# First attention of a hybrid decoder layer: values as weights in two column halves, probabilities weighed by GpSimd

## The chip, the cores and the metric

One Trainium2 chip, one core of it. The time is device microseconds of one launch; the kernel before has a median of 715.19 us over three runs (712.88 to 716.78). An engine is named as the profile names it: PE is TensorE's matrix products, PEld its weight loads, DVE is VectorE, ACT is ScalarE, POOL is GpSimd, SP is the engine whose queue issues most loads.

## The reference, cut to what matters

One decoder layer on 512 tokens of width 1024, float32. Two attention mixers read one input projection. Group 0 is a latent attention (MLA): 8 heads, head size 96 for scores and 64 for values, causal. Group 1 is a sparse attention (NSA) with a compressed, a selected and a windowed branch. Each group's 512 output features are RMS-normalised over the features of a token, both are multiplied with an output matrix and added to the residual; a squared-ReLU MLP of width 4096 follows.

```
s = einsum('bqhd,bkhd->bhqk', qi, k) * scale
p = masked_softmax(s, pos[None, :] <= qpos[:, None])
o_a = einsum('bhqk,bkhd->bqhd', p, v)            # MLA, 8 heads of 64
mix = concatenate([rms_norm(o_a, grp_norm_mla), rms_norm(o_b, grp_norm_nsa)])
x = x + mix @ w_o
h2 = rms_norm(x, ln2_g)
x = x + square(relu(h2 @ w_up)) @ w_down
```

## The kernel before, in words

The 512 tokens are four tiles of 128 (t = 0 to 3). All of the work is written out by hand for each engine, in one list per engine, with semaphores between them; nothing is scheduled by a planner. A `Signal` counts what is done, and `wait_ge(*signal.at(key))` waits for the one of that key.

Attention runs as a list of units, one unit for one query tile and one head. Units 0 to 31 are the first attention (`N_MLA = 32`; tile 0 with heads 0 to 7, then tile 1, and so on; a unit of tile t has (t+1) times 128 keys). Then come the units of the second attention; unit 32 + u is called step u here, and steps 0 to 15 are the selected and the windowed branch of query tile 3. Each engine walks over the units in a loop with index n, and does for several units at a time one stage of each:

- PE computes the score of unit n (L1630 for the first attention, L1641 and L1642 for the second), queries on partitions, keys along the row, in banks S.
- DVE adds the mask and finds the row minimum, into `s_buf` (`low_unit`, L1108), with two banks and two buffers in turn.
- ACT takes the exponential into `p_buf` and sums the row into `den` (`exp_unit`, L759), one unit later.
- PE turns the probabilities, 128 keys at a time, into a bank T (`turn_unit(n - 2)`, L1463, the same line that records every transpose).
- DVE (odd units) or ACT (even units) copies the bank into `pt_buf` (`pt_out(n - 3)`, L1118 and L769).
- PE multiplies with the values (`mix_unit(n - 4)`, L1669). The turned probabilities are the weights (keys by 128 queries) and the 64 value columns of the head are what moves; the result has queries on partitions, 8 heads beside one another in a bank O.

A float32 product is two records each of PEld and PE in the trace (transposes are one). When the eight heads of a query tile are done, DVE divides by the row sums and writes `o_mla` (`out_row("mla", t)`, L1129 to L1140).

Among the units of the first attention stand other jobs: the last projections of the second attention (`project`, L1442 to L1444, 27 units), its head norms (`norm_in` on ACT, `nsa_sum` on DVE, a power on POOL at L473 and L476, `nsa_row` and `nsa_turned` on DVE), and copies into high and low parts (`act_lo` L1224, `q_pairs` L1232). A float32 matrix is kept as two float32r parts, high and low, for dense products.

The two attentions are two loops on each engine. PE's first loop goes on for four rounds after its last score to empty its stages (L1678), and only then does the second loop begin (L1778); ACT and DVE have the same seam.

In the second attention's time group 0 of the mix is finished: ACT squares and sums `o_mla` (L854), POOL takes the power and writes the scaled `mix_row` (L575), PE turns it by four transposes (`turn_mix(0, t)`, at steps 9, 15, 20 and 23), ACT and DVE split it into `act_hi` and `act_lo` (L638, L963). From step 28 on PE multiplies it with the output matrix (`project_out`), and DVE adds the result to `x` (`residual`). SP loads `x` again for that after weight piece `X_AGAIN`.

## Time and profile before

| | |
|---|---|
| median of three runs | 715.19 us |
| the profiled execution's own time | 715.14 us |
| its span in the trace | 713.3 us |
| PE, PEld busy | 687.9, 589.8 us |
| DVE, ACT, POOL busy | 366.0, 294.8, 96.1 us |
| mean granted clock of TensorE | 0.99 |

The first attention lies at about 101 to 190 us of the span, the second at 189 to 349 us, the MLP behind 351 us. Busy time of PE is modelled and can run over a short gap, so the time that a group of products adds is better read from the chain of waits, which shows how far one group pushes the next. The profile page divides the span in 40 slices of 17.8 us.

### The profile page before, as it was taken

The page shows a single profiled execution, that of the slowest core. Times are in us where ns is not written, and L with a number is a line of the kernel's source. Part 1 is how long each engine was busy: PE and PEld are TensorE (multiplying, and loading weights), DVE is VectorE, ACT ScalarE, POOL GpSimd, SP SyncE. Part 2 cuts the span into 40 slices and gives each one's busy share as a digit, 9 for nine tenths or more (in the row PEclk, how much of TensorE's full clock was granted, in tenths as well). Part 3 has the DMA queues.
Part 4 walks back from the last instruction along what each step waited for, and adds up shares of the span by engine and source line. Part 5 has one row for each costly group of instructions (what it writes and reads, how often), then busy time and mean ns, then how long its engine had stood idle before and what let it go on. Part 6 is the DMA issues. An engine that isn't in the chain of part 4 may idle for free.

```text
span 713.3 us, 9987 instructions
## 1 busy us (share of the span) xinstructions
PE 687.9 (96%) x3703; PEld 589.8 (83%) x3703; DVE 366.0 (51%) x716; ACT 294.8 (41%) x638; POOL 96.1 (13%) x148
## 2 busy tenths in 40 slices
PE   7999999999899999898799999999999999999998
PEld 5999878887699888787698888888888888888886
DVE  5665764697665865776646444323224454432311
ACT  5554664566565642646334334212113433421110
POOL 2536653221220201022000000000000000000000
PEclk9999999999899999899999999999999999999999
DMA  7340414200205100200033332232233223323302
GB/s 284 107 141 33 122 65 145 90 31 31 68 22 207 60 30 1 90 0 31 1 119 119 102 106 89 92 115 89 88 102 105 89 89 106 101 89 95 97 1 103
DMA packets 18386, 61.63 MB, mean 86 GB/s; under 512 B 2168, under 2 KB 2296, under 8 KB 18338
## 3 DMA queue, kind: packets, MB, share of 16 engines
q1 hardware_dynamic: 17138, 57.51, 24.3%
q0 software_dynamic: 1056, 3.42, 1.5%
q8 instruction: 30, 0.49, 0.3%
q14 instruction: 18, 0.15, 0.1%
q10 hardware_dynamic: 144, 0.07, 0.0%
HBM read 58.83 MB, written 2.15 MB: 85 GB/s over the span
## 4 chain that ended last, share of the span: by engine, by line
PE 85%; DVE 8%; issue 3%; ACT 3%; POOL 1%; DMA 0%; SPq 0%; DVEq 0%; ACTq 0%; POOLq 0%
PE bank L1442 14%; PE bank L1443 14%; PE bank L1444 14%; PE bank L1771 8%; PE bank L1770 8%; PE bank L1772 8%; PE bank L1463 6%; PE bank L1669 5%; PE bank L1711 1%; PE bank L1630 1%; DVE s_buf L1108 1%; PE bank L1641 1%; PE bank L1642 1%; DVE w_lo L946 1%; DVE w_lo L949 1%
## 5 line engine op out<-in xcount | busy, mean ns | idle before, releaser
L949 DVE TENSOR_TENSOR w_lo<-raw,w_hi 128x1024 fp32r<-128x1024 f32 (+3 forms) x89 | 103.3, 1166 | 120.6 <-ACT w_hi L625 120.5
L625 ACT ACTIVATE w_hi<-raw 128x1024 fp32r<-128x1024 f32 (+3 forms) x89 | 89.1, 1008 | 123.2 <-PE bank L1444 118.2
L1770 PE MATMUL bank<-act_hi,w_hi 128*128 128x512 f32 (+3 forms) x288 | 106.8, 371 | 0.0
L1772 PE MATMUL bank<-act_hi,w_lo 128*128 128x512 f32 (+3 forms) x288 | 106.7, 370 | 0.0
L1771 PE MATMUL bank<-act_lo,w_hi 128*128 128x512 f32 (+3 forms) x288 | 106.7, 370 | 0.0
L1442 PE MATMUL bank<-w_hi,a_hi 128*128 128x512 f32 x256 | 99.6, 389 | 0.0
L1443 PE MATMUL bank<-w_lo,a_hi 128*128 128x512 f32 x256 | 99.6, 389 | 0.0
L1444 PE MATMUL bank<-w_hi,a_lo 128*128 128x512 f32 x256 | 99.6, 389 | 0.0
L1442 PE MATMUL bank<-w_hi,act_hi 128*128 128x512 f32 (+3 forms) x224 | 90.1, 402 | 2.5 <-DVE act_lo L963 2.2
L1443 PE MATMUL bank<-w_lo,act_hi 128*128 128x512 f32 (+3 forms) x224 | 80.8, 361 | 0.0
L1444 PE MATMUL bank<-w_hi,act_lo 128*128 128x512 f32 (+3 forms) x224 | 80.7, 360 | 0.0
L759 ACT ACTIVATE p_buf<-s_buf,stats 128x128 f32<-128x128 f32 (+3 forms) x96 | 53.5, 559 | 47.7 <-PE bank L1463 27.3
L1407 DVE TENSOR_TENSOR sq_b<-relu_b 128x512 f32<-128x512 f32 x32 | 22.1, 692 | 81.9 <-ACT relu_b L928 81.9
L928 ACT ACTIVATE relu_b<-bank 128x512 f32<-128x512 f32 x32 | 19.1, 598 | 106.3 <-PE bank L1772 106.3
L1770 PEld LDWEIGHTS bank<-act_hi,w_hi 128*128 128x128 f32 x288 | 54.2, 188 | 9.2
L1772 PEld LDWEIGHTS bank<-act_hi,w_lo 128*128 128x128 f32 x288 | 54.2, 188 | 9.1
L1771 PEld LDWEIGHTS bank<-act_lo,w_hi 128*128 128x128 f32 x288 | 54.2, 188 | 9.0
L1444 PEld LDWEIGHTS bank<-w_hi,a_lo 128*128 128x128 f32 x256 | 48.0, 188 | 10.1
L1442 PEld LDWEIGHTS bank<-w_hi,a_hi 128*128 128x128 f32 x256 | 48.0, 188 | 9.9
L1443 PEld LDWEIGHTS bank<-w_lo,a_hi 128*128 128x128 f32 x256 | 48.0, 188 | 9.9
L1442 PEld LDWEIGHTS bank<-w_hi,act_hi 128*128 128x128 f32 x224 | 43.0, 192 | 9.9 <-DVE act_lo L963 2.8
L1669 PE MATMUL bank<-n_v,pt_buf 128*128 128x64 f32 x320 | 45.4, 273 | 3.3 <-ACT pt_buf L769 2.0
(193 smaller groups left out, 1068.7 us busy)
## 6 DMA issues: line engine op xcount, KB each, us to landing
raw<-weights SPq DMA_DIRECT2D x86, 512.0 KB, 3.3
x<-x SPq DMA_DIRECT2D x8, 512.0 KB, 5.8
raw<-weights SPq DMA_DIRECT2D x7, 384.0 KB, 4.3
bias<-bias_by_distance POOLq DMA_DIRECT2D x1, 2048.0 KB, 9.1
y<-x SPq DMA_DIRECT2D x8, 256.0 KB, 2.2
raw<-weights SPq DMA_DIRECT2D x4, 288.0 KB, 2.8
raw<-weights SPq DMA_DIRECT2D x4, 280.0 KB, 3.1
consts<-consts SPq DMA_DIRECT2D x1, 692.0 KB, 4.2
```

The costliest lines, as they stand in the source:

```text
L625: ins = act.activation(w_hi[:, m % RING, 0:width], raw[:, n % RAW, 0:width], ACT.Copy)
L759: act.activation(p_buf[:, n % 2, 0:nk], s_buf[:, n % 2, 0:nk], ACT.Exp, scale=-1.0, bias=neg_max[:, m:m + 1], accum_out=den[:, d:d + 1]).t ...
L949: ins = dve.tensor_tensor(w_lo[:, m % RING, 0:width], raw[:, n % RAW, 0:width], w_hi[:, m % RING, 0:width].bitcast(F32), ALU.subtract)
L1407: dve.tensor_tensor(sq_b[:, f % 2, :], relu_b[:, f % 2, :], relu_b[:, f % 2, :], ALU.mult).then_inc(*sq_done.mark((half, f)))
L1442: pe.matmul(dst, a_h, w_h, start=start, stop=False)
L1443: pe.matmul(dst, a_h, w_l, start=False, stop=False)
L1444: return pe.matmul(dst, a_l, w_h, start=False, stop=stop)
L1463: ins = pe.transpose(bank[0:m, i * step:i * step + k], tile, ident[0:k, 0:k])
L1669: ins = pe.matmul(bank[:, 64 * h:64 * h + 64], pt_buf[:, n % 2, j * P:(j + 1) * P], v, start=j == 0, stop=j == t)
L1770: pe.matmul(dst, h[:, ws], act_hi[:, k, cols], start=k == 0, stop=False)
L1771: pe.matmul(dst, h[:, ws], act_lo[:, k, cols], start=False, stop=False)
L1772: ins = pe.matmul(dst, l[:, ws], act_hi[:, k, cols], start=False, stop=k == KD - 1)
```

## The change

The product with the values is turned around for the first attention alone. The 64 value columns of a head are now the weights, and the turned probabilities (keys by 128 queries) move; the result has the features on partitions. Two heads of a pair write partitions 0 to 63 and 64 to 127 of a bank O, so each uses one half of the array's columns, and the two heads' instructions alternate (`mix_pair`). One bank O holds the four pairs of a query tile.

Since a query is now a column, the division by the row sum is done before: DVE takes the reciprocal of each unit's sum (`unit_den`), and POOL multiplies the unit's probabilities with it in place (`weigh`). PE turns a unit three rounds behind its score, where it was two, and the copy is four behind; the products of a pair come five and six behind. There are four buffers for probabilities and four for turned ones.

The output needs no transposes any more: ACT copies the bank to `ot_hi` and squares it, DVE subtracts into `ot_lo`, sums the squares over the four pairs (`ot_low`); PE sums over partitions with a column of ones (`ot_squares`), DVE and POOL make the scale of it (`ot_mean`, `ot_rsqrt`), and it is applied to the output product's result in `residual`. The transposes, squares, scalings and splits of group 0 in the second attention are gone.

The two loops on each of PE, ACT and DVE are one: the second attention's first scores stand among the last products of the first. POOL's head norms, which stood in a row without anything between them, now stand between the weighings; two rotary steps move behind weighings 0 and 4; one job of ACT and DVE (`q_pairs` of tile 3) moves from unit 25 to 27. SP loads `x` again later (behind the score of step 15), since probability buffers lie in its place.

```diff
+OT_HI, OT_LO, OT_SUM, OT_MS, OT_RS = ({HEADS * t + HEADS + d: t for t in range(NT)} for d in (5, 6, 8, 9, 10))
-PAIR_QUERIES = {25: 3, N_MLA + 13: 2, N_MLA + 23: 1, N_MLA + 46: 0}
+PAIR_QUERIES = {27: 3, N_MLA + 13: 2, N_MLA + 23: 1, N_MLA + 46: 0}
-MIX_AT = {9: 0, 15: 1, 20: 2, 23: 3}
...
                 if n == X_AGAIN:
                     sp.wait_ge(*scaled.at(("nq", 0)))
+                    sp.wait_ge(*mixed.at(N_MLA - 1))
+                    sp.wait_ge(*scores.at(UNITS.index(("win", NT - 1, HEADS - 1))))
...
+            def weigh(n):
+                kind, t, h = UNITS[n]
+                p = p_of(n)[:, 0:(t + 1) * P]
+                d = h + 8 * (out_of(n) % 4)
+                pool.wait_ge(*dve_step.at(("rden", n)))
+                pool.tensor_scalar(p, p, rden[:, d:d + 1], 1.0, ALU.mult, ALU.mult).then_inc(*normed.mark(n))
...
+            for n in range(N_MLA + 1):
+                if n - 1 in HEADS_AT:
+                    rotate(*HEADS_AT[n - 1])
+                if n >= 1:
+                    weigh(n - 1)
+                if n - 2 in NORM_AT:
+                    norm_rsqrt(NORM_AT[n - 2])
+                if n in OT_RS:
+                    ot_rsqrt(OT_RS[n])
...
+            def ot_out(t):
+                n = HEADS * t + HEADS - 1
+                bank = O[t % 2].rearrange("p (c s) -> p c s", c=4)
+                act.wait_ge(*product_of(n))
+                act.activation(ot_hi[t], backwards(bank), ACT.Copy).then_inc(*ot_copied.mark(t))
+                if square_before(("mix", 0, t)):
+                    act.wait_ge(*summed.at(square_before(("mix", 0, t))))
+                act.activation(square, O[t % 2], ACT.Square).then_inc(*squares.mark(("mix", 0, t)))
...
+            def unit_den(n):
+                d = UNITS[n][2] + 8 * (out_of(n) % 4)
+                dve.wait_ge(*probs.at(n))
+                dve.reciprocal(rden[:, d:d + 1], den[:, d:d + 1]).then_inc(*dve_step.mark(("rden", n)))
+
+            def ot_low(t):
+                bank = O[t % 2].rearrange("p (c s) -> p c s", c=4)
+                dve.wait_ge(*ot_copied.at(t))
+                dve.tensor_tensor(ot_lo[t], backwards(bank), ot_hi[t].bitcast(F32), ALU.subtract).then_inc(*ot_rest.mark(t))
+                dve.wait_ge(*squares.at(("mix", 0, t)))
...
+                dve.tensor_reduce(ot_sum, by_token, AX.X, ALU.add).then_inc(*summed.mark(("mix", 0, t)))
...
-            for n in range(N_MLA, last + 9):
+            for n in range(last + 9):
+                if n - 4 >= 0 and n - 4 < N_MLA and (n - 4) % 2 == 1:
+                    pt_out(n - 4)
...
+                if n < N_MLA:
+                    mla_step(n)
+                if n >= 1 and n - 1 < N_MLA:
+                    unit_den(n - 1)
...
+            def mix_pair(n):
+                _, t, h = UNITS[n]
+                pe.wait_ge(*act_pt.at(n))
+                pe.wait_ge(*dve_pt.at(n + 1))
+                if h == 0:
+                    pe.wait_ge(*(copied.at(("nq", 2 + t)) if t < 2 else dve_step.at(("ms", t - 2))))
+                for j in range(t + 1):
+                    for i in range(2):
+                        ins = pe.matmul(O[t % 2][64 * i:64 * i + 64, P * (h // 2):P * (h // 2) + P], m_v[:, j, (h + i) * VD:(h + i + 1) * VD],
+                                        pt_of(n + i)[:, j * P:(j + 1) * P], start=j == 0, stop=j == t)
+                ins.then_inc(*mixed.mark(n + 1))
...
-            for n in range(N_MLA + 4):
-                if n < N_MLA:
-                    score_unit(n)
...
-                if n - 4 >= 0:
-                    mix_unit(n - 4)
-                if n - 2 >= 0 and n - 2 < N_MLA:
-                    turn_unit(n - 2)
...
-            for n in range(N_MLA, last + 10):
+            for n in range(last + 10):
...
                 compress(n - N_MLA)
+                if n - 5 >= 0 and n - 5 < N_MLA and (n - 5) % 2:
+                    mix_pair(n - 6)
...
+                if n - 3 >= 0 and n - 3 < N_MLA:
+                    turn_unit(n - 3)
```

PE's list at the end of the first attention, before: L1630 is a first-attention score, L1669 the product with the values, L1463 on `p_buf` the transposes of one unit, L1641 and L1642 the second attention's scores.

```order
L1630 MATMUL bank<-m_k,m_q 128x512
L1669 MATMUL bank<-m_v,pt_buf 128x64 x4
L1463 MATMUL bank<-consts,p_buf 128x128 x4
L1669 MATMUL bank<-m_v,pt_buf 128x64 x4
L1463 MATMUL bank<-consts,p_buf 128x128 x4
L1669 MATMUL bank<-m_v,pt_buf 128x64 x4
L1463 MATMUL bank<-consts,p_buf 128x128 x4
L1669 MATMUL bank<-m_v,pt_buf 128x64 x8
L1641 MATMUL bank<-act_hi,q_pairs_101 128x512
L1642 MATMUL bank<-act_lo,q_pairs_101 128x512
L1463 MATMUL bank<-consts,raw_row 128x128 x2
```

The same place of the changed kernel: L1722 is the first-attention score, L1770 a pair's product, L1555 a transpose, L1733 and L1734 the second attention's scores, L1777 the sum over partitions.

```order
L1722 MATMUL bank<-m_k,m_q 128x512
L1555 MATMUL bank<-consts,p_buf 128x128 x4
L1733 MATMUL bank<-act_hi,q_pairs_112 128x512
L1734 MATMUL bank<-act_lo,q_pairs_112 128x512
L1555 MATMUL bank<-consts,raw_row 128x128 x2
L1770 MATMUL bank<-pt_far,m_v 64x128 x8
L1555 MATMUL bank<-consts,p_buf 128x128 x4
L1777 MATMUL bank<-stats,ot_sum 128x1
L1733 MATMUL bank<-act_hi,q_pairs_112 128x512
L1734 MATMUL bank<-act_lo,q_pairs_112 128x512
L1555 MATMUL bank<-consts,p_far 128x128 x4
L1733 MATMUL bank<-act_hi,q_pairs_112 128x512
```

After the last first-attention score, five products and three groups of transposes stood ahead of the next score; now one group of transposes stands there, and products, transposes and new scores alternate.

POOL's list for the last three head norms, before: L473 and L476 are the two instructions of one norm, L554 belongs to what follows the first attention.

```order
L473 TENSOR_SCALAR stats<-stats 128x8
L476 TENSOR_TENSOR stats<-stats 128x8
L473 TENSOR_SCALAR stats<-stats 128x8
L476 TENSOR_TENSOR stats<-stats 128x8
L473 TENSOR_SCALAR stats<-stats 128x8
L476 TENSOR_TENSOR stats<-stats 128x8
L554 MEMSET v_diag 128x512
```

The same norms in the changed kernel: L521 and L524 are the norm, L606 is `weigh`, L611 is `ot_rsqrt`.

```order
L606 TENSOR_SCALAR p_buf<-p_buf,stats 128x384 x2
L521 TENSOR_SCALAR stats<-stats 128x8
L524 TENSOR_TENSOR stats<-stats 128x8
L611 TENSOR_TENSOR stats<-stats 128x1
L606 TENSOR_SCALAR p_mid<-p_mid,stats 128x384 x2
L606 TENSOR_SCALAR p_buf<-p_buf,stats 128x384
L521 TENSOR_SCALAR stats<-stats 128x8
L524 TENSOR_TENSOR stats<-stats 128x8
L606 TENSOR_SCALAR p_buf<-p_buf,stats 128x384
L606 TENSOR_SCALAR p_mid<-p_mid,stats 128x384 x2
L521 TENSOR_SCALAR stats<-stats 128x8
L524 TENSOR_TENSOR stats<-stats 128x8
```

Each norm now stands behind a weighing and ahead of the next one, on one engine that takes its instructions in order.

DVE's list in rounds 30 to 32 of the changed kernel: L1181 is `low_unit`, L1294 `act_lo`, L1326 `unit_den`, L1332 and L1337 `ot_low`, L1018 the low part of a weight piece, L1191 the copy of a turned unit.

```order
L1181 ISA s_buf,stats<-bank,consts 128x512
L1181 ISA stats 128x1
L1294 TENSOR_TENSOR act_lo<-n_k,act_hi 64x2x128 x4
L1326 RECIPROCAL stats<-stats 128x1
L1332 TENSOR_TENSOR ot_lo_86<-bank,ot_hi_82 128x512
L1337 TENSOR_REDUCE ot_sum<-square 128x128
L1018 SCALAR_TENSOR_TENSOR w_lo<-raw,consts,w_hi 128x512 x2
L1191 COPY pt_far<-bank 128x512
L1181 ISA s_buf,stats<-bank,consts 128x512
```

Before, `act_lo` and `w_lo` stood next to each other there; the reciprocal and the two instructions of `ot_low` are what has come between two scores' `low_unit`.

## Rows read from the trace of the kernel before

**Rows 1.** Stretches: length, busy us (count) per engine, granted clock, DMA share, GB/s

```profile
104.00:148.00 44.00, 43.48 (x264) 37.63 (x263) 26.89 (x80) 22.58 (x70) 14.80 (x19) 1.00 0.33 110
148.00:180.00 32.00, 30.89 (x211) 25.36 (x209) 26.84 (x68) 22.38 (x57) 3.67 (x4) 1.00 0.05 18
195.00:240.00 45.00, 44.38 (x343) 41.90 (x341) 29.01 (x78) 26.84 (x69) 7.04 (x15) 1.00 0.30 106
```

**Rows 2.** Chain of waits: start us, us, what; first attention

```profile
111.75 0.17 PE bank L1669 x2
...
131.05 0.39 PE bank L1669 x4
...
149.83 0.61 PE bank L1669 x6
...
196.53 0.84 PE bank L1669 x8
```

**Rows 3.** Timeline of PE around the only products in column quarters: start us, us

```profile
39.30 1.03 PE L1542 MATMUL bank<-onehot,consts 33*8 33x512 f32 x8
40.27 0.87 PE L1463 MATMUL bank<-consts,c_row 128*128 128x128 f32 x6
```

**Rows 4.** Timeline of PE around a product with 64 weight columns

```profile
234.23 0.50 PE L1463 MATMUL bank<-consts,p_buf 128*128 128x128 f32 x3
234.66 0.33 PE L1606 MATMUL bank<-consts,hid_k 128*64 128x64 f32 x2
234.92 0.45 PE L1641 MATMUL bank<-act_hi,q_pairs 128*128 128x384 f32 x1
```

**Rows 5.** Stretches of the seam between the two attentions

```profile
179.96:194.73 14.77, 12.88 (x75) 11.30 (x76) 9.93 (x24) 6.74 (x17) 5.31 (x13) 0.77 0.22 69
182.90:184.84 1.94, 0.06 (x1) 0.00 (x0) 1.89 (x5) 0.62 (x1) 0.00 (x0) 1.00 0.18 30
186.90:193.70 6.80, 6.80 (x26) 5.83 (x26) 4.08 (x12) 2.31 (x7) 4.49 (x12) 0.50 0.15 50
```

**Rows 6.** Chain of waits at the seam

```profile
182.16 1.41 DVE w_lo L946 x2
...
184.84 1.10 PE bank L1669 x8
```

**Rows 7.** Timeline of POOL: a rotary step, two powers, a scaling of 512 columns

```profile
103.19 2.64 POOL L527 TENSOR_TENSOR rope_t<-qk_row,tab_k 128x128 f32<-128x128 f32 x2 [3.24 <-DVE qk_row L1060]
...
111.78 1.66 POOL L527 TENSOR_TENSOR rope_t<-qk_row,tab_k 128x128 f32<-128x128 f32 x2 [5.13 <-DVE qk_row L1060]
...
153.36 1.64 POOL L476 TENSOR_TENSOR stats<-stats 128x8 f32<-128x8 f32 x1
...
202.68 0.69 POOL L575 TENSOR_SCALAR mix_row<-o_mla,stats 128x512 f32<-128x512 f32 x1
```

**Rows 8.** Groups of DVE by line, 148 to 182 us: busy, mean ns, idle before

```profile
L1224 DVE TENSOR_TENSOR act_lo<-n_k,act_hi 64x256 fp32r<-64x256 f32 x16 | 6.7, 418 | 0.2
...
L1140 DVE TENSOR_TENSOR o_mla<-bank,stats 128x512 f32<-128x512 f32 x2 | 1.4, 692 | 0.1
...
L1211 DVE TENSOR_SCALAR gates<-gates 128x24 f32<-128x24 f32 x4 | 0.7, 177 | 3.7 <-ACT gates L777 3.6
...
L1131 DVE RECIPROCAL stats<-stats 128x8 f32<-128x8 f32 x2 | 0.4, 203 | 0.1
```

**Rows 9.** Chain of waits at a transpose of group 0, and at a split of it

```profile
206.22 0.45 PE bank L1463 x4
...
244.01 0.53 DVE act_lo L963
```

**Rows 10.** Issue and landing of `x`, step 15's score, the next piece's split

```profile
214.00 1.99 SPq L452 DMA_DIRECT2D x<-x  x4
...
DMA to landing us min/median/max: 4.3/5.7/7.0
...
223.69 0.47 PE L1641 MATMUL bank<-act_hi,q_pairs 128*128 128x512 f32 x1
...
237.42 1.32 ACT L623 ACTIVATE w_hi<-raw,consts 128x512 fp32r<-128x512 f32 x2
```

## What is predicted, before the changed kernel has run

> **What bounds the kernel now.** I read the page first: PE is busy for 687.9 of 713.3 us at a mean clock of 0.99. So a gain must come from PE's own work, or from the few places where PE waits or runs slowly. The stretches by time come next [rows 1]. From 104 to 148 us PE is full (43.48 of 44 us) and DVE is at 61%: PE alone sets the pace. From 148 to 180 us PE (30.89 of 32) and DVE (26.84 of 32) are both nearly full, and what one saves the other may keep. From 195 to 240 us PE is full again (44.38 of 45). Between them lies the seam, where PE's first loop empties its stages before the second attention's scores begin. Its stretch, from the product of unit 27 to the score of step 4, is 14.77 us long, with DVE busy for 9.93 us; PE stands for 1.9 us of it, and then runs 6.8 us at half clock [rows 5]. The chain of waits names DVE's copies ahead of that pause, and a product of 1.10 us behind it [rows 6].
>
> **The products in halves.** Before, a unit's product pushes the chain by 0.17, 0.39, 0.61 and 0.84 us for tiles 0 to 3 [rows 2]. A pair costs twice that, and there are four pairs a tile: 4 x 2 x 2.01 = 16.1 us. Afterwards a pair has (t+1) products per head with 128 moving columns. A record of 128 float32 columns costs PE 0.11 us (four transposes are 0.45 us [rows 9]), a product is two records, and two heads make 0.44 us per 128 keys one after the other, or 0.22 us if the two column halves run at once. For that question the trace has one place: eight records in four column quarters, six of 512 columns and two of 112. At 0.11 us for 128 columns they are 2.8 us of work; the next instruction starts 0.97 us behind their first [rows 3]. So column parts do overlap, in float32 too, there with only 33 rows. I take 0.22. To that comes what a visit to another column shape costs. The product with 64 weight columns starts 0.10 us after the transposes ahead of it should be over (234.23 + 3 x 0.11 = 234.56, start 234.66), has two records of 0.055 us, and the next score starts 0.15 us after their end [rows 4]. That is 0.25 us per pair. A pair is then 0.25 + 0.22 (t+1) = 0.47, 0.69, 0.91, 1.13 us, and sixteen are 12.8 us. PE saves 3.3 us, none of it in tiles 0 and 1 (4.6 us against 4.5), all of it in tiles 2 and 3.
>
> The Trainium skill (TensorEngine Tiling (Array Packing), Tiling Modes, Key Properties) says that a change of the tiling mode, other than a change of the tile, drains TensorE, and promises up to twice the speed for a dimension of 64. The 0.25 us of rows 4 agrees with the first. By the promise alone the pairs would be half of 16.1 us, 8 us; with a drain sixteen times it is the sum above.
>
> **The first attention up to the seam.** In rounds 17 to 29 PE loses four pairs of tile 2 (0.31 us each) and one of tile 3 (0.55): -1.8 us. DVE gains work there: about twelve reciprocals, which I price at the 0.20 us of eight columns [rows 8] (nothing to 0.20 are the ends), 2.4 us; two `ot_low`, a subtraction and a sum of 512 columns at 0.69 each (as L1140, which has a bank as its input too), 2.8 us; two `ot_mean` at 0.18, 0.4 us; and loses two `out_row`, 0.18 + 0.20 + 0.69 each, 2.1 us. That is +3.5 us on an engine with 5.2 us of idle time in the stretch, 3.6 of it waits for the gates from ACT [rows 1, 8]. Moving the queries' copies from unit 25 to 27 takes two jobs of DVE out of the worst round, where they follow four of `act_lo` at 0.42 us each [rows 8]. All ends together run from -3 (PE's saving and the smoother order show, DVE's work is hidden) to +4 us (DVE's work shows in full and the norms' wait, below, comes on top). I take 0, as both engines are nearly full and their changes have opposite signs. ACT gains 1.2 us per tile (a copy and a square of 512 columns) with 9.6 us free in the stretch: hidden.
>
> **Weighing on POOL.** A multiplication by a column over 512 columns is the same instruction as `mix_row`: 0.69 us [rows 7]. 32 units with 0.69 us as the upper end are 22 us, on an engine that is busy for 14.8 of 44 and 3.7 of 32 us. The way of one unit is longer by the reciprocal and the weighing, 0.9 us, and by one more copy behind DVE's other jobs; against that stands one more round of 2.1 to 2.9 us. So the turn itself waits no more than before. Priced at nothing. If that cover fails, it is rival 2.
>
> **The seam.** Before, five products and three groups of transposes stood between the last first-attention score and the next score; now new scores stand among them. At full clock PE's content of the 14.77 us is, counted from the code, five products at 0.84, 27 transposes at 0.11 and 8 score records at 0.21 (512 columns of float32r, twice the price of 128 float32 columns): 8.9 us, and 7.7 with the products as pairs and one sum over partitions. DVE's content is 9.93 us, plus four reciprocals (0.8), one `ot_low` (1.4), one `ot_mean` (0.2), less one `out_row` (1.1): 11.2 us. DVE is the longer, and round 30 is its lump (`act_lo`, then `ot_low`, then `w_lo`, some 5.4 us between two scores' minima). I take 11.5 us, so -3.3. The ends are -7.0 (PE's 7.7 alone) and 0 (DVE's lump stops PE, and its clock falls, as before).
>
> **The second attention.** Four groups of transposes of `mix_row` go, 0.45 us each, -1.8 us [rows 9]; two of the four sums over partitions stand there instead, 0.21 us each as two records at the price of rows 2: net -1.4. All but the last of these are in a stretch where PE is full [rows 1]. DVE loses four splits; one is on the chain of waits for 0.53 us [rows 9]: -0.5. ACT loses 5.6 us which nobody waits for. The scale in `residual` is one instruction as before: 0. The load of `x` moves from 214.0 to the score of step 15 at 223.7. It lands 7.0 us later at the latest, at 231, with the next weight piece close behind; ACT splits that piece at 237.4 [rows 10]. Five microseconds of cover, so 0; without them ACT, and the exponentials behind that split, would wait.
>
> **Sum.** 0 - 3.3 - 1.4 - 0.5 = -5.2 us on the profiled execution's own 715.14 us: 709.9 us. The median of the runs, 715.19, is the same within 0.05.
>
> **Rival 1: the halves do not overlap** with 128 rows and full partitions, unlike the 33 rows of rows 3. A pair then costs 0.25 + 0.44 (t+1), sixteen are 21.6 us, 8.8 more than forecast. The 2.6 us in tiles 0 and 1 show in full; of the 6.2 in tiles 2 and 3 perhaps half, since DVE sets the pace there. That is 709.9 + 5.7 = 715.6 us. Against it: rows 3.
>
> **Rival 2, slower: the head norms wait behind the weighings.** POOL takes its list in order, and each norm stands behind a weighing that DVE releases only at the end of a round. DVE wants the power two or three jobs of some 0.7 us later. POOL then needs 0.5 to 0.69 for the weighing, 0.2 and 1.64 for the power of eight columns [rows 7]: 2.4 us against 1.5 to 2.1. If POOL is slowed as the first of the two rotary steps was, 2.64 against 1.66 us, it is 3.9 us and DVE stands 2 us per norm, the next weighing too. Where DVE is full, nothing takes that up: five norms lie in or near such rounds, 10 us, and the three early ones 0.5 us each. 709.9 + 11.5 = 721.4 us. It decides from the point where a weighing takes some 1.1 us. Against it: in the rounds of tile 1 DVE is early and stands anyway, and there it would cost nothing.
>
> The Trainium skill (GPSIMD Engine Reference, Specifications) says that GpSimd shares its SBUF interfaces with VectorE, with contention from VectorE's instructions with two SBUF inputs. The slow rotary step ran beside such ones; the fast one did in part as well, so the trace does not settle it. By that rule the stretched case of this rival is the likelier one, but only while `act_lo`, `w_lo` and the norm's products run.
>
> **Rival 3: the seam gives nothing back.** PE still pauses at DVE's lump and its clock falls to half for 6.8 us there or a little earlier, which costs 3.4 us [rows 5]. For it: PE now has less work against a fuller DVE. 709.9 + 3.3 = 713.2 us.
>
> **How the numbers follow.** Forecast (706 to 712) 0.54; better than 706, with the seam on PE's own time, 0.07; rival 1 0.07; rival 2 0.13; rival 3 0.19. Half a per cent is 3.6 us, about what a measurement of this kernel can tell from no change: faster is below 711.6, slower above 718.8. Faster takes all of the first two but little and a part of rival 3, 0.61; slower is most of rival 2 and its neighbourhood, 0.14; the rest, 0.25, is the same. The range from 702 to 718 holds all of rivals 1 and 3 and leaves rival 2 out. The likeliest case alone is 706 to 712.
>
> **What would show it.** The pair's products: 8 units of keys in tile 3 should push the chain by some 1.1 us a pair; 2.0 us is rival 1. The wait of DVE's `nq_row` for POOL's power, and the mean of `weigh` at 512 columns (0.69, against 1.1), show rival 2. The seam should have no pause of PE over 1 us and a granted clock of 1.00 in the 15 us behind the last first-attention score; half clock there is rival 3. No transposes of `mix_row` at 205 to 245 us, and no wait of ACT for `raw` near 235 us. The forecast is wrong as a whole if the first attention, up to its last score, ends over 3 us earlier or later than at 179 us.

## The result

The changed kernel takes 721.1 us (median of 18 runs, 717.98 to 725.63) against 716.81 us for the kernel before on the same chip (18 runs): ratio 1.0062, 95% interval 1.0042 to 1.0082. The forecast was 709.9 us, range 702 to 718. It was wrong, and on the wrong side. The profiled execution took 719.58 us with a span of 717.6 us, 4.3 us more than before.

### The profile page after: what moved, and what is told of

Read it like the earlier page. It is cut to its first block, busy times and chain, and to the rows that moved or that the text cites. A ratio compares the mean times of both kernels' runs of the same rounds, so it can differ in the third digit from the quotient of the medians.

```text
span 717.6 us, 10026 instructions
## 1 busy us (share of the span) xinstructions
PE 683.9 (95%) x3695; PEld 579.0 (81%) x3695; DVE 369.9 (52%) x745; ACT 293.9 (41%) x634; POOL 109.9 (15%) x172
## 4 chain that ended last, share of the span: by engine, by line
PE 81%; DVE 8%; ACT 4%; issue 4%; POOL 2%; DMA 0%; DVEq 0%; ACTq 0%; SPq 0%; POOLq 0%
PE bank L1534 14%; PE bank L1536 14%; PE bank L1535 14%; PE bank L1861 8%; PE bank L1863 8%; PE bank L1862 8%; PE bank L1555 5%; PE bank L1758 3%; PE bank L1802 1%; DVE s_buf L1181 1%; PE bank L1733 1%; PE bank L1734 1%; POOL stats L524 1%; PE bank L1722 1%; DVE w_lo L1018 1%
## 5 line engine op out<-in xcount | busy, mean ns | idle before, releaser
L1534 PE MATMUL bank<-w_hi,act_hi 128*128 128x512 f32 (+3 forms) x192 | 76.5, 399 | 2.8 <-DVE act_lo L1035 2.5
L1535 PE MATMUL bank<-w_lo,act_hi 128*128 128x512 f32 (+3 forms) x192 | 68.0, 354 | 0.0
L1536 PE MATMUL bank<-w_hi,act_lo 128*128 128x512 f32 (+3 forms) x192 | 67.9, 354 | 0.0
L835 ACT ACTIVATE p_buf<-s_buf,stats 128x128 f32<-128x128 f32 (+3 forms) x80 | 44.6, 558 | 33.5 <-DVE stats L1181 17.2
L1758 PEld LDWEIGHTS bank<-n_v,pt_buf 128*128 128x128 f32 x320 | 43.2, 196 | 6.6 <-DVE pt_buf L1191 3.4
```

Source lines behind the costliest of these rows:

```text
L835: act.activation(p_of(n)[:, 0:nk], s_buf[:, n % 2, 0:nk], ACT.Exp, scale=-1.0, bias=neg_max[:, m:m + 1], accum_out=den[:, d:d + 1]).then_i ...
L1534: pe.matmul(dst, a_h, w_h, start=start, stop=False)
L1535: pe.matmul(dst, a_h, w_l, start=False, stop=False)
L1536: return pe.matmul(dst, a_l, w_h, start=False, stop=stop)
L1758: ins = pe.matmul(bank[:, 64 * h:64 * h + 64], pt_of(n)[:, j * P:(j + 1) * P], v, start=j == 0, stop=j == t)
```

## The profile after

The page of the changed kernel, part 1, and the row of the granted clock in part 2:

```profile
PE 683.9 (95%) x3695; PEld 579.0 (81%) x3695; DVE 369.9 (52%) x745; ACT 293.9 (41%) x634; POOL 109.9 (15%) x172
...
PEclk9999999999999999999999999999999999999999
```

PE is busy for 4.0 us less than before and yet the span is longer: what the products saved did not shorten it. Stretches of the changed kernel (columns as in [rows 1]), the same three and the seam between them:

```profile
104.00:148.00 44.00, 42.61 (x251) 33.56 (x250) 27.94 (x95) 22.79 (x70) 21.60 (x36) 1.00 0.29 102
148.00:180.00 32.00, 27.30 (x193) 20.51 (x191) 26.60 (x72) 21.19 (x54) 11.84 (x17) 1.00 0.07 23
180.00:195.00 15.00, 11.33 (x88) 8.80 (x88) 12.28 (x33) 9.27 (x23) 8.22 (x18) 0.89 0.22 70
195.00:240.00 45.00, 43.16 (x334) 39.91 (x333) 27.03 (x73) 22.52 (x56) 1.57 (x3) 1.00 0.30 109
```

From 148 to 180 us PE now stands for 4.7 us (1.1 before), from 195 to 240 us for 1.8 (0.6 before). What PE waited for from 136 to 206 us (us in total, times, longest):

```profile
PE bank L1555 <- DVE pt_far L1191: 4.7, 3, 2.0
PE bank L1770 <- DVE pt_far L1191: 2.7, 1, 2.7
PE bank L1555 <- DVE tap_planes L1350: 1.5, 2, 0.8
PE bank L1555 <- DVE pt_buf L1191: 0.9, 1, 0.9
PE bank L1733 <- DVE act_lo L1294: 0.7, 1, 0.7
```

L1555 records the transposes, L1770 the pair's products, L1733 the second attention's scores. All five lines name DVE. From 100 to 250 us DVE in turn stood 7.1 us for the powers of the head norms, which POOL computes, in six waits (before: 2.1 us, in one). Two of its groups of waits from 136 to 206 us, the changed kernel first and then the kernel before:

```profile
DVE nq_row L1246 <- POOL stats L524: 4.1, 3, 2.0
```

```profile
DVE gates L1211 <- ACT gates L777: 3.6, 2, 2.3
```

Four places in the order of work tell where the time went. The numbers are starts of a unit's score in us (step 16 is unit 48):

| | score of unit 31 | step 4 | step 16 | end of span |
|---|---|---|---|---|
| before | 178.89 | 194.76 | 227.15 | 713.3 |
| after | 182.04 | 196.13 | 230.50 | 717.6 |
| difference | +3.15 | +1.37 | +3.35 | +4.3 |

So the first attention lost 3.15 us; from there to step 4 1.78 us came back; by step 16 1.98 us were lost again; and 0.95 us after that (0.90 of it by step 28). Up to unit 15 the two kernels are within 0.25 us of each other. Unit 21 is 0.63 us late, unit 25 4.25 us.

## The experiments

The table has every kernel that was timed. The last column takes out one source of scatter. Over the runs of one kernel the time lies on a straight line against TensorE's mean granted clock (0.976 to 0.999, slopes of 390 to 650 us per unit of clock, residuals of 0.2 to 0.7 us); the column is that line's value at a clock of 0.99 (called "at one clock" below). It ran to 716.0, 716.2 and 716.0 us for the kernel before in three of the four batches measured with the experiments, and to 715.9 us in the fourth without two executions that lie far off the line. As an estimate from these residuals and batches, values that differ by less than about 0.5 us are not told apart. The positions come from one profiled execution each, and each has its own stretches of low clock, so differences of 1 to 2 us between two of them can be clock alone.

| kernel | median us | ratio to before (95%) | unit 31 | step 4 | step 16 | at 0.99 |
|---|---|---|---|---|---|---|
| changed kernel | 721.1 | 1.0062 (1.0042 to 1.0082) | 182.04 | 196.13 | 230.50 | 719.4 |
| e1, norms' powers earlier | 719.24 | 1.0035 (1.0006 to 1.0065) | 179.03 | 193.08 | 227.46 | 717.0 |
| e2a, no weighing | 714.9 | 0.9978 (0.9954 to 1.0003) | 178.58 | 192.26 | 226.64 | 716.0 |
| e2b, nor reciprocals | 716.44 | 1.0004 (0.9977 to 1.003) | 178.11 | 191.88 | 226.25 | 715.6 |
| e3, before with joined loops | 710.45 | 0.992 (0.9891 to 0.995) | 178.92 | 190.33 | 222.58 | 712.6 |
| e6a, short sum over chunks | 717.86 | 0.9999 (0.9976 to 1.0022) | 180.13 | 194.75 | 228.84 | 717.0 |
| e7, changed, loops apart | 724.12 | 1.0123 (1.0088 to 1.0158) | 182.18 | 200.24 | 233.86 | 721.5 |
| b1, three edits | 715.74 | 0.9984 (0.9959 to 1.0009) | 178.39 | 189.48 | 223.76 | 714.3 |
| e4, output's jobs later | 717.96 | 1.0027 (0.9995 to 1.0059) | 182.26 | 195.13 | 229.28 | 717.2 |
| e5, pair not alternating | 720.35 | 1.0058 (1.003 to 1.0086) | 182.72 | 197.00 | 231.86 | 720.5 |
| b2, sum on TensorE | 713.78 | 0.9975 (0.9945 to 1.0004) | 177.84 | 191.38 | 225.94 | 715.1 |
| e10, joined, queries later | 709.2 | 0.9902 (0.9867 to 0.9937) | 177.65 | 189.19 | 221.43 | 711.7 |
| b3, b1 and tile 3 later | 712.14 | 0.9944 (0.9917 to 0.9972) | 178.46 | 190.90 | 224.54 | 713.9 |

### The norms behind the weighings (e1)

```
-                if n - 2 in NORM_AT:
-                    norm_rsqrt(NORM_AT[n - 2])
+                if n - 1 in NORM_AT:
+                    norm_rsqrt(NORM_AT[n - 1])
```

> The changed kernel, with one thing moved: on GpSimd each head norm's power stands one round earlier in the list, right behind the weighing of the unit before, where before it stood behind one more weighing. Theory 1 (the norms wait behind the weighings): VectorE's products with the norms' scales waited 7.1 us for these powers, in waits up to 2.4 us. If this is what built the loss of units 21 to 25, the score of unit 25 comes 2 to 4 us earlier than in the changed kernel (it is at 166.3 us there) and the time is 717 to 719 us (ratio to the kernel before 1.001 to 1.003). Theory 2 (VectorE has more work than the rounds of tile 2 hold, and who waits for whom is secondary): within 0.7 us of the changed kernel, 721 us, ratio 1.006. A weighing would now wait behind the power in the same round; if that costs as much as it saves, the waits of TensorE for probabilities' turns grow and the time is also 721.

The score of unit 25 came 1.9 us earlier (164.34), that of unit 31 3.0 us; at one clock the kernel gains 2.4 us. The mechanism is in two timelines of the changed kernel. POOL first, then DVE, from 155.8 us (start us, us, idle time before and what ended it):

```profile
156.10 0.58 POOL L606 TENSOR_SCALAR p_buf<-p_buf,stats 128x384 f32<-128x384 f32 x1 [1.02 <-DVE stats L1326]
156.77 0.20 POOL L521 TENSOR_SCALAR stats<-stats 128x8 f32<-128x8 f32 x1
157.06 1.65 POOL L524 TENSOR_TENSOR stats<-stats 128x8 f32<-128x8 f32 x1
```

```profile
155.85 0.16 DVE L1326 RECIPROCAL stats<-stats 128x1 f32<-128x1 f32 x1
156.21 0.56 DVE L1181 CUSTOM_DVE_ANT_0 s_buf<-bank,consts 128x384 f32<-128x384 f32 x1 [0.20 <-PE bank L1722]
...
158.74 0.69 DVE L1246 TENSOR_TENSOR nq_row<-n_q,stats 128x512 f32<-128x512 f32 x1 [1.96 <-POOL stats L524]
```

POOL stood for 1.0 us for a reciprocal that DVE computes at the end of its round, then needed 0.58 + 0.20 + 1.65 us. DVE came for the power one job (a minimum, 0.56 us) after the reciprocal, and stood 1.96 us. In e1 the same wait is 0.36 us:

```profile
156.48 0.69 DVE L1246 TENSOR_TENSOR nq_row<-n_q,stats 128x512 f32<-128x512 f32 x1 [0.36 <-POOL stats L524]
```

Theory 1 holds for this part; over 136 to 206 us DVE's waits for these powers fall from 4.1 to 0.4 us. The run's median shows less of it (719.24 us, ratio 1.0035, just above theory 1's 717 to 719 us). In the profiled run PE's clock was half for some ten microseconds from 244 us, and what e1 had gained until then (3.0 us at step 16) was gone at step 28.

### Without the weighing, and without the reciprocals (e2a, e2b)

```
-                if n >= 1:
-                    weigh(n - 1)
...
-                pe.wait_ge(*(normed if kind == "mla" else probs).at(n))
+                pe.wait_ge(*probs.at(n))
```

> The changed kernel without GpSimd's 32 weighings; the reciprocals stay on VectorE, TensorE turns the probabilities as soon as ScalarE has written them. Left out: the division of the first attention by its denominators. Theory 1 (the weighings are the cause, by delaying the norms and the turns): all of the loss in the first attention goes, the last first-attention score comes at 179 us or before and the time is 709 to 713 us, ratio 0.990 to 0.995. Theory 2 (VectorE's work is the cause): VectorE has the same work, so little comes back: 719 to 721 us, ratio 1.003 to 1.006.

```
-                dve.reciprocal(rden[:, d:d + 1], den[:, d:d + 1]).then_inc(...)
```

> The changed kernel without the weighings and without the 32 reciprocals on VectorE, whose wait for the exponential stays. Left out: the division of the first attention. Theory 1: as without the weighings alone, since the reciprocals are only 0.15 us each: within 1.5 us of that kernel. Theory 2 (VectorE full): another 2 to 4 us on top of what leaving out the weighings brings, since 16 reciprocals of 0.15 us go in units 16 to 31, where VectorE sets the pace, and 32 in all are 4.9 us.

Without the weighings the score of unit 31 comes at 178.58 us, 3.5 us earlier and where theory 1 put it; but the time is 714.9 us, where theory 1 said 709 to 713 and theory 2 719 to 721. So both are wrong on the total: the first attention's loss is gone and with it only part of the whole. At one clock all weighings together cost 3.4 us (719.4 to 716.0); e1 gets 2.4 us back by moving the norms. Leaving out the 32 reciprocals gives 0.4 us more, not 2 to 4, and 0.4 us is within the scatter. And even with neither, the wait at the seam is unchanged. PE's longest wait from 136 to 206 us in e2a:

```profile
PE bank L1768 <- DVE pt_far L1189: 2.7, 1, 2.7
```

### The join alone (e3), and the changed kernel without it (e7)

e3 takes the kernel before and runs each engine's two loops as one (`for n in range(last + 10)` on PE, with the bodies of both). e7 takes the changed kernel and walks over the rounds twice, first for the first attention's stages alone.

> The kernel before, with its two loops on TensorE, ScalarE and VectorE joined into one, so that scores of the second attention are issued among the last products and turns of the first; everything else as before. Theory 3 (joining gives the seam's 3.3 us back where VectorE has no added work there): 711 to 713 us, ratio 0.993 to 0.996, and the score of step 4 comes 3 us earlier than at 194.7 us. Rival (VectorE's and ScalarE's lump around unit 30 stops TensorE there whatever the loops are, and its clock falls in either case): ratio 0.999 to 1.001.

> The changed kernel with its loops taken apart again at the seam: TensorE, ScalarE and VectorE empty the first attention's stages before the second attention's first score, as in the kernel before. The jobs of tile 3's output stay in rounds 37 to 42. Theory 3 (the join is worth some 3 us in the changed kernel too, as it was when it was made alone on the kernel before): 724 to 725 us, ratio 1.010 to 1.012. Rival (in the changed kernel the join gives nothing, since the pair's product behind VectorE's lump of round 30 stops TensorE in either case): within 1 us of 721 us.

e3 beats both kernels: 0.992 of the time before. Its step 4 comes 4.4 us earlier. Stretch and PE's waits from 180 us on in e3:

```profile
180.00:195.00 15.00, 14.22 (x111) 12.48 (x112) 12.90 (x32) 10.18 (x26) 4.80 (x13) 1.00 0.21 61
```

```profile
PE bank L1625 <- DVE act_lo L1216: 0.8, 1, 0.8
PE bank L1447 <- DVE gates L1287: 0.6, 1, 0.6
```

And the same stretch of the kernel before:

```profile
180.00:195.00 15.00, 13.11 (x77) 11.53 (x78) 10.03 (x25) 6.97 (x18) 5.31 (x13) 0.77 0.22 71
```

In e3 PE is busy for 14.22 of 15 us at full clock, before for 13.11 us at 0.77. At one clock e3 gains 3.4 us (716.0 to 712.6). Undoing the join in the changed kernel costs 3.4 us at step 16 and 2.1 us at one clock; PE then waits 4.4 us in one piece for a copy of DVE (of 5.2 us in two). So the join is worth about what the forecast gave the seam, and the rest of the change takes it away again: from the score of unit 31 to that of step 16 it is 48.3 us before, 51.7 in e7 (the rest without the join) and 48.5 in the changed kernel.

### What lies in the seam (e4, e6a)

DVE in the changed kernel behind the last minima of the first attention, and PE beside it:

```profile
182.23 1.84 DVE L1294 TENSOR_TENSOR act_lo<-n_k,act_hi 64x256 fp32r<-64x256 f32 x4
184.10 0.16 DVE L1326 RECIPROCAL stats<-stats 128x1 f32<-128x1 f32 x1
184.19 0.67 DVE L1332 TENSOR_TENSOR ot_lo<-bank,ot_hi 128x512 fp32r<-128x512 f32 x1
184.77 1.03 DVE L1337 TENSOR_REDUCE ot_sum<-square 128x128 f32<-128x512 f32 x1
185.73 1.40 DVE L1018 SCALAR_TENSOR_TENSOR w_lo<-raw,consts,w_hi 128x512 fp32r<-128x512 f32 x2
187.05 0.68 DVE L1191 COPY pt_far<-bank 128x512 f32<-128x512 f32 x1
```

```profile
184.53 0.40 PE L1734 MATMUL bank<-act_lo,q_pairs 128*128 128x512 f32 x1
184.76 0.38 PE L1555 MATMUL bank<-consts,raw_row 128*128 128x128 f32 x2
187.88 1.09 PE L1770 MATMUL bank<-pt_far,m_v 128*64 128x128 f32 x16 [2.74 <-DVE pt_far L1191]
188.90 1.05 PE L1555 MATMUL bank<-consts,p_buf 128*128 128x128 f32 x4
189.75 0.43 PE L1777 MATMUL bank<-stats,ot_sum 128*128 128x1 f32 x2
190.03 0.77 PE L1733 MATMUL bank<-act_hi,q_pairs 128*128 128x512 f32 x1
```

The copy stands behind 4.8 us of jobs, 1.5 of them new (`ot_lo`, `ot_sum`). The pair needs the copies of both its units, and PE's list holds the turns and scores behind it. PE stands for 2.74 us, and then works at a lower clock, 0.63 over these 4 us, so that four transposes take 1.05 us for 0.66:

```profile
188.00:192.00 4.00, 4.00 (x29) 3.53 (x29) 2.56 (x9) 2.17 (x6) 3.21 (x9) 0.63 0.36 131
```

It is the lump of [rows 6] again, one stage later.

```
-OT_HI, ... = ({HEADS * t + HEADS + d: t for t in range(NT)} for d in (5, 6, 8, 9, 10))
+OT_HI, ... = ({HEADS * t + HEADS + d + (0, 3, 2, 0)[t]: t ...} for d in (5, 6, 8, 9, 10))
```

> The changed kernel; only the rounds of the output's jobs (ScalarE's copy and square, VectorE's subtraction and sum over chunks, the product with ones and the power) change: tile 1 three rounds later, tile 2 two rounds later, tiles 0 and 3 as they were. Theory 2b (what hurts is that these jobs stand in rounds 22 and 30, where VectorE is fullest; in round 30 they make the pair's copy late and TensorE wait 2.7 us at the seam): that wait falls below 1 us, the score of step 4 comes 2 to 3 us earlier than in the changed kernel, and the time is 717 to 719 us, ratio 1.001 to 1.004. Rival (the lump only moves): within 0.7 us of the changed kernel, ratio 1.006.

```
-                dve.tensor_reduce(ot_sum, by_token, AX.X, ALU.add)...
+                dve.tensor_copy(ot_sum, square[:, 0:P])...
```

> The changed kernel, with VectorE's sum over four chunks (0.94 to 1.03 us, four times) cut to a copy of the first chunk (about 0.2 us). Left out: three quarters of the mean square of the first attention's output. It takes 0.8 us of VectorE out of rounds 14, 22, 30 and 38. If VectorE's work in the full rounds 22 and 30 is what sets the pace there, 1 to 1.6 us of the total come back, 719.5 to 720 us, ratio 1.004 to 1.005; if the waits for GpSimd's powers set it, less than 0.5 us.

e4's time (717.96 us; 2.2 us less at one clock) is what theory 2b says, but two of its signs did not come: the wait shrinks only from 2.7 to 1.6 us, not below 1, and step 4 comes 1.0 us earlier, not 2 to 3. Unit 31 is as late as in the changed kernel, but the profiled e4 ran at half clock for 3.4 us near 156 us, where the changed kernel has full clock, so its positions do not tell how the 2.2 us divide between the first attention and the seam. e6a gives 2.4 us for some 3.2 us of DVE's time, more than the 1 to 1.6 expected. Unit 31 comes 1.9 us earlier: the sum of round 22 lies in the full rounds before it, and ScalarE's next square waits for it too (2.7 us once, at 162.16 us; 2.0 us in e6a). DVE's added work did count, but the output's jobs far more than the reciprocals.

### Do the column halves overlap (e5)

```
-                for j in range(t + 1):
-                    for i in range(2):
+                for i in range(2):
+                    for j in range(t + 1):
```

> The changed kernel, with a pair's products issued head by head: all key tiles of the first head in the left column half, then all of the second in the right, so that neighbouring records share a half. Theory 4 (two column halves run at once only when neighbouring products are in different halves): the 16 records of a pair of tile 3 take about 1.8 to 2.0 us for 1.05 us, those of tile 0 0.6 for 0.45; in tiles 0 and 1, where TensorE sets the pace, 0.22 x 4 and 0.44 x 4 = 2.6 us are lost, in tiles 2 and 3 perhaps half of 6.2 us: 725 to 727 us, ratio 1.011 to 1.014. Rival (the pair's low price comes from the 64 columns of weights, not from an overlap): no change, 721 us, records as before.

A pair of tile 3 alternating (changed kernel), then head by head (e5):

```profile
180.53 1.09 PE L1770 MATMUL bank<-pt_far,m_v 128*64 128x128 f32 x16 [0.22 <-issue]
```

```profile
180.73 1.56 PE L1770 MATMUL bank<-pt_far,m_v 128*64 128x128 f32 x16
```

From a pair's first record to the start of the next instruction it is 0.37, 0.59, 0.81 and 1.03 us in tiles 0 to 3 of the changed kernel, and 0.37, 0.60, 1.08 and 1.49 us in e5. In tile 0, with one key tile, the two orders are the same list, so e5 tests nothing there. With two key tiles nothing changes; from three on alternating does pay. Even 1.49 us is less than the 1.9 us of halves one after the other (0.15 + 0.44 x 4), so the halves still overlap in part. The rival (no change of the records) is refuted, and the theory's 4 to 6 us did not come either: the pairs of tiles 2 and 3 take 2.9 us more in all, of which 1.1 us shows at one clock and nothing in the medians (720.35 to 721.1). Tiles 0 and 1 lose nothing, and in tiles 2 and 3 PE has waits for DVE that a longer product can fill; this last reason is argued, not tested.

### Mending the change (b1, b2, b3) and the join (e10)

b1 is e1 and e4 and one more edit: ScalarE writes the squares with the four chunks of a token side by side.

```
-  act.activation(square, O[t % 2], ACT.Square)...
+  act.activation(square.rearrange("p (s c) -> p c s", c=4), bank, ACT.Square)...
```

> The changed kernel with three edits together: each norm's power one round earlier on GpSimd; the output's jobs of tiles 1 and 2 three and two rounds later; ScalarE writes the squares of the output with the four chunks side by side, so that VectorE's sum over them reads neighbours (0.69 us for 0.97 us if the stride is what makes it slow; ScalarE's write with a stride may become slower instead). If the edits add up (2.4 + 2 + 0.6 us at one clock): 716 to 717 us, ratio 0.999 to 1.001. If the later places of the output's jobs gain nothing: as with the norms alone, ratio 1.003.

> The changed kernel with the norms' powers one round earlier, the output's jobs of tiles 1 and 2 later, and the sum over the four chunks taken from VectorE: ScalarE writes the squares in reversed order of tokens, and TensorE multiplies each of the four chunks with the column of ones, into one sum (four products of one column for one, two rounds earlier). VectorE loses 0.97 us four times; TensorE gains three products of 0.1 to 0.2 us, four times, 1.2 to 2.4 us in all. If VectorE sets the pace in rounds 17 to 34, that is better than the combination with the squares side by side (715.7 us): 713 to 715 us, ratio 0.995 to 0.998. If TensorE pays in full what VectorE saves: 716 us, ratio 0.999.

> The combination of three edits (norms' powers earlier, the output's jobs of tiles 1 and 2 later, squares side by side; 715.7 us), and the output's jobs of tile 3 moved from rounds 37, 38, 40, 41, 42 to 38, 40, 42, 43, 44. In round 37 ScalarE's copy and square (0.6 and 1.2 us) stand ahead of its copies of the taps, and TensorE waits 1.2 us there for VectorE's part of these. If that is the loss of the seam that is left, the scores of steps 5 to 9 come 1 us earlier and the time is 714 to 715 us, ratio 0.995 to 0.998. If the jobs only stand in the way of other taps (round 39 has some too), as before: 715 to 717 us, ratio 0.998 to 1.000.

> The kernel before with its loops joined (710.5 us), and the copies of the first queries for the second attention two rounds later (unit 27 for 25), as in the changed kernel: this part of the change alone, on top of the join. If it takes work out of the worst round of VectorE (round 26), the score of unit 27 comes up to 1 us earlier and the time is 709.5 to 710.5 us, ratio 0.990 to 0.992. If it only shifts the work towards the seam, 710.5 to 712 us, ratio 0.992 to 0.994.

In b1 the edits give 5.1 us at one clock, about their sum. b2's median (713.78 us) lies where its first case put it, but at one clock it is no better than b1 (715.1 to 714.3), so the gain expected from relieving VectorE is not shown. b3 is 0.9944 of the time before, but at one clock it is only 0.4 us better than b1, which is within the scatter; its lower median is mostly the clock (mean 0.991 to 0.988). The expected microsecond is there in the trace: the wait of 1.20 us for DVE's taps behind step 6 is gone, and from step 4 to step 9 it is 13.1 us for 14.4. It does not reach step 9, because the profiled b3 came to step 4 1.4 us later than b1, with half clock for 3.4 us of the seam (0.86 for 1.00 from 178.4 to 190.9 us), and 0.7 us of it is given back between steps 9 and 11. e10 is the fastest kernel of all, 0.9902 (711.7 us at one clock): unit 27 comes 1.3 us earlier than in e3, as expected from a less full round 26 of DVE, and 1.2 us of it are left at step 16. No kernel with the new products beats the joined kernel before: at one clock the best is 713.9 us, against 712.6 in e3.

## Why the prediction was wrong

The sum had 0 for the first attention, -3.3 us for the seam and -1.9 us for the second attention, -5.2 in all. The profiled executions have +3.15, -1.78 and +2.93, +4.3 in all. All three terms failed, none by the price of the products.

**The products in halves: right, slightly better.** A pair was to take 0.47 to 1.13 us and takes 0.37 to 1.03; sixteen take 11.2 us for 12.8 forecast and 16.1 before. Rival 1 is refuted. The Trainium skill (TensorEngine Tiling (Array Packing), Tiling Modes, Key Properties) says that a change of the tiling mode drains TensorE. The trace has a fixed part of 0.15 us a pair, for which 0.25 was taken; that fits the rule and does not prove it, and it bore little on the outcome.

**The first attention up to the seam: 0 was forecast, +3.15 us measured.** This is the first step that failed: the ends were -3 to +4, and I chose the middle because PE gains and DVE loses. But PE's gain was worth nothing where DVE sets the pace, and DVE had new waits beside its new work. Between the scores of units 17 and 31:

```profile
140.89:178.89 38.00, 36.94 (x259) 31.43 (x257) 30.98 (x78) 26.51 (x68) 5.90 (x6) 1.00 0.09 29
```

```profile
141.88:182.04 40.16, 35.24 (x255) 26.87 (x254) 33.40 (x92) 26.82 (x69) 16.47 (x23) 1.00 0.08 27
```

DVE's busy time (the third pair) rose by 2.4 us and its idle time stayed at some 7 us. Before, 3.6 us of that were waits for the gates, which the forecast counted as room; now 4.1 us are waits for POOL's powers. e1, which takes these away, is at 37.1 us for the same stretch. e1 takes 3.0 us away at unit 31, e6a 1.9 and e1 and e4 with the cheaper sum 3.65 (b1), so the two causes overlap: each is a delay in the same full list. The prediction priced DVE's reciprocals at 2.4 us in these rounds (32 of them give 0.4 us, e2b) and `ot_low`'s sum at 0.69 us, where it takes 1.04 (1.9 us at unit 31, e6a). It also counted two `ot_low` in rounds 17 to 29, where by `OT_LO` only round 22 has one (the others are 14, 30 and 38): its +3.5 us of work should have been +2.1.

The prediction's own sign of being wrong as a whole, this attention ending over 3 us from 179 us, was met by a hair (182.04).

**Weighing on POOL: nothing was forecast, 3.4 us measured** (e2a, at one clock). Rival 2 named the right mechanism and the wrong point. It was to decide from a weighing of 1.1 us. The weighing takes 0.58 us at 384 columns and 0.69 at 512, and the wait came all the same: in the timeline above DVE wants the power one job (0.56 us) after it releases the weighing, and not 1.5 to 2.1 us. Its price was too high, 11.5 us for the 2.4 that e1 gets back. That its total, 721.4 us, is the measured 721.1 is chance: the rest of the loss has other causes. The stretched weighing exists: 1.65 us at 144.94 us for 0.58 and 1.46 at 104.33 us for 0.37, each beside a `w_lo` of DVE (raw and `w_hi` in), and in e1 1.11 us at 156.43 us beside `nq_row`. The Trainium skill (GPSIMD Engine Reference, Specifications) names contention with VectorE's instructions with two SBUF inputs, and these three agree with it. Not every such meeting stretches: a weighing at 175.72 us ran 0.37 us beside a `w_lo` and took its usual 0.69, and one at 108.35 us took 0.72 for 0.37 with DVE idle. In all three of the 32 weighings are stretched in the changed kernel, and six in e1.

**The seam: -3.3 us was forecast, -1.8 us measured** from unit 31 to step 4, and even that flatters it: the products stand one or two rounds further back than before, so the last pair (1.22 us with its change of column shape) is now behind the score of step 4. With it the seam gives back only 0.6 us. The join gives its 3.4 us (e7, at step 16), and e3 shows 4.4 at step 4 without the rest of the change. Rival 3 is half true: PE pauses for 2.7 us where none over 1 us was expected, and its clock falls, though for less: 0.79 over the 8 us from 186 us on, for half clock over 6.8 us before [rows 5]. The prediction knew the lump (some 5.4 us) and counted it as busy time of DVE, 11.2 us in all; it did not ask which instruction of PE stands behind it.

**The second attention: -1.9 us was forecast, +2.0 us measured** between step 4 and step 16, and +0.95 behind that. With the two together this is the largest miss, and the prediction had terms only for what goes away. The gaps between PE's instructions in the two traces add up to nearly all of the 2.0 us. The last pair of the first attention is here now: +1.22. The waits for DVE's copies of the taps grow: from one of 0.62 us to three of 0.76, 0.77 and 0.31, +1.4 in all. The sum over partitions for tile 3 adds 0.23. Two groups of transposes are gone: -0.44 each, as forecast.

```profile
197.60 0.44 PE L1555 MATMUL bank<-consts,raw_row 128*128 128x128 f32 x2 [0.76 <-DVE tap_planes L1350]
197.96 1.09 PE L1770 MATMUL bank<-pt_far,m_v 128*64 128x128 f32 x16
...
204.06 0.44 PE L1555 MATMUL bank<-consts,raw_row 128*128 128x128 f32 x2 [0.77 <-DVE tap_planes L1350]
```

The second of these waits comes from the output's jobs, which the prediction counted in the seam or as hidden. In round 37 ScalarE's copy (L878) and square (L881) stand ahead of its copies of the taps (L924), and DVE then waits for these; ScalarE first, then DVE:

```profile
201.77 0.59 ACT L878 ACTIVATE ot_hi<-bank 128x512 fp32r<-128x512 f32 x1
202.25 0.60 ACT L881 ACTIVATE square<-bank 128x512 f32<-128x512 f32 x1
202.73 0.78 ACT L924 ACTIVATE tap_planes<-bank 64x256 f32<-64x256 f32 x2
```

```profile
203.13 0.88 DVE L1350 COPY tap_planes<-bank 64x256 f32<-64x256 f32 x2 [1.39 <-ACT tap_planes L924]
```

b3, which moves these jobs, has no wait of PE there, where b1 has 1.20 us. Of the 0.95 us behind step 16 most can be one stretch of half clock, 247.0 to 250.4 us, 1.7 us, where the kernel before has full clock; against it stand the other two groups of transposes. The cover for the load of `x` held: ACT has no wait for `raw` from 225 to 250 us.

**The clock.** At one clock the change costs 3.4 us, over the runs as they fell 4.3. The mean over 18 runs is 0.986 in the changed kernel and 0.987 to 0.990 in the batches of the kernel before. That the change lowers the clock is not shown: the batches of one kernel differ by as much.

## What to carry to other kernels

Work saved on the engine that is 95% busy is worth nothing in the stretch where another one sets the pace: price each stretch by the engine that its waits name, and find the instruction that waits behind a lump of jobs, not only the lump's size. When a helper engine takes over a step in a list that it works through in order, compare when the next user wants its result with when the new step's input is released, job by job. When a stage moves back by some rounds, look for the work that crosses from one stretch of the sum into the next, so that it is priced once. Test the parts alone: here the join of two loops, one part of the change, beats the whole by 1.4% (1.0% at one clock).

## What was not expected of the hardware

Here a reduction with a stride cost more on VectorE, and a write with a stride on ScalarE. The sum over four chunks takes 1.01 to 1.07 us in the changed kernel, where the chunks are 128 elements apart, and 0.68 side by side in b1; ScalarE's square takes 0.60 us in order and 1.08 with neighbours written 4 elements apart. Both in b1:

```profile
L881 ACT ACTIVATE square<-bank x4: 1074/1082/1197, 131.6 to 195.4; 128x512 f32<-128x512 f32 x4
L1337 DVE TENSOR_REDUCE ot_sum<-square x4: 673/676/678, 136.9 to 199.6; 128x128 f32<-128x512 f32 x4
```

(min, median and max in ns.) VectorE saves 0.36 us a time, ScalarE pays 0.48.

The same short pauses of PE can be followed by short or long stretches at half clock, or by none. After pauses of 1.3 and 0.8 us near 242 us, TensorE in e1 ran at half clock from 244 to 254 us, at full busy time (first row, 0.62 as it takes in two microseconds of full clock); in the changed kernel the same pauses, near 245 us, were followed by 3.4 us at half clock (the other two rows). And after one and the same pause of 1.19 us at 182.6 us b1 kept its full clock and b3 lost it for 3.4 us. What decides between them no run here shows:

```profile
246.00:256.00 10.00, 10.00 (x54) 9.13 (x53) 5.79 (x18) 4.51 (x12) 0.00 (x0) 0.62 0.00 0
```

```profile
247.00:250.00 3.00, 3.00 (x16) 3.00 (x16) 1.88 (x9) 2.84 (x6) 0.00 (x0) 0.51 0.13 52
250.00:253.00 3.00, 3.00 (x23) 2.76 (x23) 2.71 (x8) 1.88 (x6) 0.00 (x0) 0.92 0.00 0
```
